# Row maxima, weight split and gate pieces in another order in a two-block transformer kernel

## The reference, cut to what matters

```
proj = rmsnorm(x) @ w_in                    # front columns, then 2 * 1024 gate columns
# mixer A: 8 heads on the 64 keys with the highest index score
score = where(causal, sum_h w_i * relu(q_i @ k_i.T), -inf)
idx   = top_k(score, 64)
o_a   = softmax(q_a @ k_a[idx] * scale + bias) @ v_a[idx]
# mixer B: 8 heads, three branches (compressed, selected, window), each with its gate
o_b   = g0 * softmax(q_b @ kc.T + bias) @ vc + g1 * softmax(q_b @ ks.T + bias) @ vs + g2 * (... kw, vw)
mix   = sigmoid(gate_a) * (o_a @ w_branch_a) + sigmoid(gate_b) * (o_b @ w_branch_b)
x     = x + mix @ w_out
```

## Time and profile before

| | us |
|---|---|
| three runs | 997.29, 998.59, 1000.55 |
| median | 998.59 |
| the profiled execution, its own time | 998.59 |
| its span in the trace | 996.8 |
| TensorE busy | 969.5 (97%) |
| VectorE busy | 576.7 (58%) |
| ScalarE busy | 495.0 (50%) |

### The profile page before, as it was taken

One profiled execution on the slowest core, in us unless ns is written; L12 is line 12 of the kernel. 1 busy time (PEld: TensorE's weight loads), 2 busy tenths in 40 slices (PEclk: granted clock), 3 DMA queues, 4 the chain that ended last, 5 costly groups with the idle time before them and its releaser, 6 DMA issues.

```text
span 996.8 us, 12359 instructions
## 1 busy us (share of the span) xinstructions
PE 969.5 (97%) x4788; PEld 779.8 (78%) x4788; DVE 576.7 (58%) x851; ACT 495.0 (50%) x686; POOL 5.7 (1%) x13
## 2 busy tenths in 40 slices
PE   6999999999999998999999999999999999999996
PEld 5777888888878875888888888877777788888885
DVE  5654756655356455475665437578874676545434
ACT  5664644434345564454444335556675464435332
POOL 0000000000000000000000001000000000000000
PEclk9999999999999998999999999999999999999998
DMA  9624545555445420454554548533224455545551
GB/s 324 213 86 148 208 172 190 189 174 195 180 169 177 161 85 1 172 209 168 195 184 172 225 174 313 193 132 127 85 96 158 169 172 185 191 170 190 196 184 42
DMA packets 25924, 168.76 MB, mean 169 GB/s; under 512 B 2792, under 2 KB 3798, under 8 KB 6679
## 3 DMA queue, kind: packets, MB, share of 16 engines
q1 hardware_dynamic: 24647, 163.57, 45.9%
q0 software_dynamic: 1232, 4.57, 1.2%
HBM read 167.05 MB, written 1.08 MB: 169 GB/s over the span
## 4 chain that ended last, share of the span: by engine, by line
PE 93%; DVE 3%; ACT 2%; DMA 1%; issue 1%; SPq 0%; ACTq 0%; DVEq 0%
PE ps L1437 79%; PE ps L1553 1%; PE ps L2033 1%; PE ps L1735 1%; PE ps L2044 1%; DMA x_sb<-in_x 1%; PE ps L2063 1%; PE ps L2132 1%; PE ps L1798 1%; PE ps L1627 1%; PE ps L1618 1%; PE ps L1513 1%; PE ps L1590 1%; PE ps L1856 1%; PE ps L1667 1%
## 5 line engine op out<-in xcount | busy, mean ns | idle before, releaser
L871 DVE TENSOR_TENSOR w_both<-raw,w_both 128x2048 fp32r<-128x2048 f32 x150 | 342.0, 2285 | 210.3 <-ACT w_both L409 210.2
L1437 PE MATMUL ps<-w_both,a_hi 128*128 128x512 f32 (+1 forms) x1536 | 416.0, 393 | 3.2 <-DVE m_lo L909 1.9
L409 ACT ACTIVATE w_both<-raw 128x2048 fp32r<-128x2048 f32 x150 | 286.4, 1916 | 188.8 <-DMA raw<-in_down 43.5
L1437 PEld LDWEIGHTS ps<-w_both,a_hi 128*128 128x128 f32 x1536 | 282.2, 189 | 63.7 <-issue 9.3
L1437 PE MATMUL ps<-w_both,a_lo 128*128 128x512 f32 (+1 forms) x768 | 235.6, 388 | 0.0
L1437 PEld LDWEIGHTS ps<-w_both,a_lo 128*128 128x128 f32 x768 | 143.9, 188 | 30.4
L1437 PE MATMUL ps<-w_both,h_hi 128*128 128x512 f32 x576 | 158.3, 396 | 0.0
L1437 PEld LDWEIGHTS ps<-w_both,h_hi 128*128 128x128 f32 x576 | 107.5, 188 | 25.6
L1437 PE MATMUL ps<-w_both,h_lo 128*128 128x512 f32 x288 | 90.5, 395 | 0.0
L1437 PE MATMUL ps<-w_both,m_hi 128*128 128x512 f32 x256 | 72.1, 404 | 2.3 <-ACT projA L490 1.4
L587 ACT ACTIVATE mlp_a<-ps,tiny 128x256 f32<-128x256 f32 x44 | 18.5, 471 | 98.2 <-PE ps L1437 98.2
(11 more groups left out here) (239 smaller groups left out, 686.3 us busy)
## 6 DMA issues: line engine op xcount, KB each, us to landing
raw<-in_a_gu SPq DMA_DIRECT2D x22, 1024.0 KB, 4.8
raw<-in_b_gu SPq DMA_DIRECT2D x22, 1024.0 KB, 4.8
raw<-in_up SPq DMA_DIRECT2D x16, 1024.0 KB, 4.8
raw<-in_down SPq DMA_DIRECT2D x16, 1024.0 KB, 4.8
raw<-in_a_down SPq DMA_DIRECT2D x11, 1024.0 KB, 4.8
raw<-in_b_down SPq DMA_DIRECT2D x11, 1024.0 KB, 4.7
raw<-in_front SPq DMA_DIRECT2D x8, 1024.0 KB, 5.1
raw<-in_gates SPq DMA_DIRECT2D x8, 1024.0 KB, 4.8
```

The costliest lines, as they stand in the source:

```text
L409: A_(ring(w_hi, us)[:, 0:n], ring(raw, us)[:, 0:n], ACT.Copy).then_inc(s_hi, 1)
L871: V.tensor_tensor(ring(w_lo, us)[:, 0:n], ring(raw, us)[:, 0:n], ring(w_hi, us)[:, 0:n].bitcast(fp32), ALU.subtract).then_inc(s_lo, 1)
L1437: ins = MM(ps[:, b + T, 0:wd], chT(parts[ap_], c, T), wp[wp_][:, off:off + wd], start=(c == first and pn == 0), stop=(c == last and pn == 2))
```

## The change

Four things move; no instruction is added or removed, and the line numbers behind the first edit on VectorE are shifted by one or two.
- ScalarE splits unit gates+2 ahead of the exponentials of the compressed scores, not behind them.
- VectorE does its half of that split, and two search rounds, ahead of pair 0's row maxima: the third round moves from the middle of the compressed softmax to behind it, the fourth comes from pair 1, and the split comes from behind pair 0's maxima.
- The other four rounds stand at pairs 0 to 3, not 2 to 5.
- TensorE does one gate piece behind the values at pairs 1, 2, 4, 5, 6, 8, 9 and 10; the number of pieces per pair is the same as before.

```diff
--- before.py
+++ after.py
@@ -753,9 +753,9 @@
             q_copy(14, ch(TT, 12, 2), 4, 1.0)
             front_block("front_a", 0, U0["front_a"] + 2, 0)
             q_copy(15, ch(TT, 14, 2), 7, 1.0)
+            split_hi(U0["gates"] + 2)
             act.wait_ge(s_clm, 1)
             A_(pc_v, pc_v, ACT.Exp).then_inc(s_cex, 1)
-            split_hi(U0["gates"] + 2)
 
             def gate_block(b):
                 act.wait_ge(s_mm, U0["gates"] + 2 * b + 2)
@@ -1259,7 +1259,7 @@
             ins.then_inc(s_cau, 1)
             split_lo(U0["gates"] + 1)
             dve.wait_ge(s_cau, 1)
-            for _k in range(2):
+            for _k in range(TOPS_AHEAD // 2):
                 replaced = top_taken(top_found())
 
             dve.wait_ge(s_clg, 1)
@@ -1278,8 +1278,6 @@
             link(V.tensor_reduce(cmx, pc_v, AX.X, ALU.max))
             link(V.tensor_scalar(cmx, cmx, -1.0e20, None, ALU.max))
             V.tensor_tensor(pc_v, pc_v, per_row(cmx), ALU.subtract).then_inc(s_clm, 1)
-            for _k in range(2, TOPS_AHEAD):
-                replaced = top_taken(top_found())
             dve.wait_ge(s_cex, 1)
             link(V.tensor_reduce(csum, pc_v, AX.X, ALU.add))
             link(V.tensor_scalar(csum, csum, 1.0e-30, None, ALU.max))
@@ -1288,6 +1286,9 @@
             link(V.tensor_tensor(crec.rearrange("p (t n) -> p t n", t=2), crec.rearrange("p (t n) -> p t n", t=2),
                                  gb.rearrange("p (t n) -> p t n", t=2)[:, :, 0:8], ALU.mult))
             V.tensor_tensor(pc_v, pc_v, per_row(crec), ALU.mult).then_inc(s_cp, 1)
+            split_lo(U0["gates"] + 2)
+            for _k in range(TOPS_AHEAD // 2, TOPS_AHEAD):
+                replaced = top_taken(top_found())
             for p in range(n + 3):
                 if p < n:
                     u = CAUSAL_PAIRS[p]
@@ -1306,8 +1307,6 @@
                     found = top_found()
                     if k + 1 < TOP_STEPS[p]:
                         replaced = top_taken(found)
-                if p == 0:
-                    split_lo(U0["gates"] + 2)
                 if p - 1 in GATE_SPLIT:
                     split_lo(U0["gates"] + GATE_SPLIT[p - 1])
                 if p < n:
@@ -2086,7 +2085,7 @@
             left = list(range(7, 32))
             for p in range(n):
                 pair_transposes(p)
-                first, then = PIECES.get(p, (2, 0))
+                first, then = PIECES.get(p, (1, 1))
                 for _k in range(first):
                     gate_piece(left.pop(0))
                 pair_values(p)
@@ -2185,9 +2184,9 @@
 INDEX_BANK = (6, 4, 5)
 GATE_EMPTY = {2: 0, 5: 1, 9: 2, 13: 3}
 GATE_SPLIT = {1: 3, 3: 4, 5: 5, 7: 6, 9: 7, 10: 8, 11: 9}
-TOP_STEPS = {p: 1 for p in range(1, 6)}
-TOPS_AHEAD = 3
-PIECES = {0: (1, 0), 1: (3, 0), 2: (3, 0)}
+TOP_STEPS = {0: 1, 1: 1, 2: 1, 3: 1}
+TOPS_AHEAD = 4
+PIECES = {0: (1, 0), 1: (2, 1), 2: (2, 1), 3: (2, 0), 7: (2, 0), 11: (2, 0)}
 assert TOPS_AHEAD + sum(TOP_STEPS.values()) == S // 4 // 8
```

## The result

| | before | changed |
|---|---|---|
| median of nine runs, us | 999.53 | 1004.84 |
| lowest to highest | 995.64 to 1000.83 | 1002.56 to 1008.28 |
| profiled execution: span | 996.8 | 1002.2 |
| mean granted clock | 0.994 | 0.994 |

The ratio is 1.0067, 95% interval 1.0049 to 1.0086: the change makes the kernel about 0.7% slower. It is not the quotient of the two medians, 1.0053: 24 runs of the changed kernel are on record, from 1002.56 to 1008.38 us with a mean of 1005.5, and single runs of either kernel lie up to 5 or 6 us apart. 1006.6 us was forecast, with 1003.0 to 1009.8.

The account below looks back on a forecast made before the run. TensorE, busy 969.5 of 996.8 us, was taken to set the end. Wait 4.75, next wait 0.15, joints 1.7, late copy 0.1 and clock 1.3 sum to 8.0 us on 998.6: 1006.6 us, range 1003.0 to 1009.8.

Parts of the forecast that it names:

- The wait: Ahead of pair 1's logits: TensorE waits 4.75 us for VectorE's late row maxima of pair 0.
- The next wait: Ahead of pair 2's logits: TensorE waits for pair 1's maxima, 0.15 us more, at most 0.3.
- The joints: Gate pieces split around the values at 8 pairs: 0.24 us each with logits behind, 0.13 without, 1.7 in all.
- The sign that the prediction gave for this stretch: From pair 0's transposes to the first branch product: 1.5 to 2.5 us more than before.
- The rival of free joints: Gate pieces at all pairs: a piece costs the same anywhere, so 1004.9 us in total; chance 0.14.
- The late copy at pair 4: Values at pair 4: one piece covers too little of ScalarE's copy behind a split, a wait of 0.1 us.
- The clock: Behind the hole ahead of pair 1's logits: the granted clock falls, costing 1.3 us, ends 0 and 3.4.
- the row's 1.6: Loss read from the profile before at 380.40 to 384.00 us: a hole, then 3.40 us at clock 0.50.
- the third rival: Gate pieces at all pairs: joints are free by the skill's page, so 1004.9 us in total; chance 0.14.
- The first rival: Gate pieces' new places hide TensorE's weight-load gaps and give back 4.4 us: 1000.5 us, not slower; chance 0.05.
- the second: Pair 1's logits: the wait for pair 0's maxima doesn't come, only the joints count, 1000.4 us; chance 0.07.
- the fourth: ScalarE's work no longer fits before the copies ahead of the values; 8 pairs wait 0.5 us more each: 1010.6; chance 0.08.

Follow-up runs that it names:

- The split alone: Kernel before with only the split of unit gates+2 moved ahead, on ScalarE and VectorE: wait of 2.03 us at pair 1; pair 0's logits to its transposes 14.81 us.
- the rounds alone: Kernel before with only the search rounds moved ahead of pair 0's maxima: waits of 0.81 us at pair 1 and 1.44 at pair 2.
- the hole filled: Changed kernel plus 20 matmuls that nobody reads ahead of pair 1's logits: 1005.54 us; with such matmuls in the memory attention too, 1000.59 us.
- part 2 alone: Kernel before with only the new table of gate pieces: 999.21 against 996.87 us, ratio 1.0008; with unread matmuls in the memory attention, 996.08 against 994.92 us.
- the keepers: 20 unread matmuls in four holes of the memory attention: kernel before 995.33 us, ratio 0.9978; in the last set 994.92, changed kernel 1002.87 us.
- part 1 alone: Changed kernel with the old table of gate pieces: ratio 1.0077 to the kernel before; A (pair 0's logits to its transposes) 19.04 us, wait 4.81.
- the set without the other spread: Last set, unread matmuls in the memory attention of all four kernels: before 994.92 us, changed 1002.87, changed with hole filled 1000.59, new piece table only 996.08.

## Why the prediction was right, and where it was off

**The wait** (4.75 us forecast, 4.82 measured). Every step of the working is in the new timeline: from ScalarE's split to its exponentials 1.80 (1.81), from the softmax to the split 1.47 (1.46), the split 2.20 (2.21), the two rounds 2.75 (2.75), the maxima 1.19 (1.19). The point that carried it is that VectorE's queue is in order and stood 1.6 us ahead of TensorE, so that all beyond that was paid in full. The split alone and the rounds alone gave the waits that the same sum gives, 2.0 and 0.8.

**The next wait** (0.15 forecast) did not show. The low clock behind the hole held TensorE back by more than that. With the hole filled, at full clock, there are 0.2 us between the last queries and pair 2's logits that the old kernel does not have there (691.34 to 692.07, 0.73 against 0.53); that is the term, hidden in the changed kernel.

**The joints** (1.7 forecast, 1.07 measured with the 0.13 wait in it; 1.16 in whole time). This is the term that was mis-sized. At pairs 1 and 2 a split group costs the forecast 0.24 (4.53 against 4.29 for three pieces), at pair 4 0.35 with the wait. At pairs 5, 6 and 8 it costs 0.02 to 0.04: what follows there is the mask product, which uses the full array, so that the two pieces cost only 0.12 to 0.14 more and the product, behind a piece, gives back 0.1. The prediction took these three for pairs with logits behind, though the mask product stands between. At pairs 9 and 10 the next transposes give back 0.06 of 0.14. Together 0.48 + 0.35 + 0.08 + 0.16 = 1.07. The sign that the prediction gave for this stretch, 1.5 to 2.5 us more, failed. The rival of free joints is refuted too: the stretch grew by 1.05 us with part 2 alone, and the whole time by 1.16 with the keepers in. "TensorE: Matmul & The Clock Gate" ("Wait — 56ns, not 53.3ns?") of the Trainium skill gives the spacing of matmuls in a row, by which a piece is estimated at 1.29 us. That is below the least of all spacings of pieces measured, 1.36, and lone pieces take up to 1.60.

**The late copy at pair 4** (0.1 forecast). The values start at 719.45 where the piece alone would let them at 719.32, just behind a copy that ends at 719.40. ScalarE's timeline:

```profile
716.73 1.91 ACT L409 ACTIVATE w_both<-raw 128x2048 fp32r<-128x2048 f32 x1
718.53 0.87 ACT L770 ACTIVATE pb<-ps 128x384 f32<-128x384 f32 x2
```

and TensorE's:

```profile
717.75 1.17 PE L1436 MATMUL ps<-w_both,a_hi 128*128 128x512 f32 x4
718.76 0.62 PE L1436 MATMUL ps<-w_both,a_lo 128*128 128x512 f32 x2
719.45 0.65 PE L2059 MATMUL ps<-pct,cw 15*64 15x256 f32 x4
```

**The clock** (1.3 forecast from 0 to 3.4; 1.58 in the profile, 2.28 over the runs). The mechanism was right and the size drawn low. The reason given for taking less than the row's 1.6, that the fall may lie partly in the hole, need not hold: with the keepers a fall inside the hole was followed by a low clock for the whole of the next 5 us, at a cost of 2.6 (6.88 against 4.25 from pair 1's logits to pair 2's). In part 1 alone the clock fell just ahead of the end of the hole as well (0.93 in the microsecond before it), and the cost was 1.5 (A 19.04, less 12.71 and the wait of 4.81). What decides between the two is open.

**The sum** was 8.0; the changed kernel costs 7.5 by its stretches and 7.95 in the set without the other spread. That it comes so close is in part luck: the joints were put 0.6 too high, the low clock 0.3 to 1.0 too low. By the plain medians the change costs only 5.3 us (1004.84 less 999.53), and 1004.84 is nearest to the 1004.9 of the third rival, whose mechanism the runs refute. Such medians depend on how many low stretches the memory attention had in the runs that were drawn; of the single runs only the mean clock is on record. The first rival (time given back at the joints) and the second (no wait) are refuted; of the fourth (cover too thin) only the 0.13 at pair 4 is true.

## What to carry to other kernels

Where one engine has no wait in a stage, a reordering of the others has no wait to remove there; find each engine's slack at the places where the full one takes its results, and price the reordering by what exceeds that slack. Slack is spent once, so two moves that are cheap alone can be dear together. And a hole in a matmul stream can be paid with more than its length, as the one of 4.8 us was here and the one of 2.0 was not: look at the granted clock in the stretch behind it, and at small waits elsewhere that do the same. Matmuls whose results nobody reads, put into such holes, gave back 2.3 us at the one and 2.2 at the four.

## What the runs showed of the hardware that was not expected

A stage with four holes of 0.9 to 1.7 us within 11 us decides the spread of a program of 1000 us: without its low clock the runs of the kernel before lie within 1.5 us, with it within 7. The mean clocks agree: of the 23 runs, those at 0.998 took 994.00 to 995.68 us and those at 0.991 took 999.93 to 1000.88. The same busy time led to different clocks: 1.47 us busy of 3.20 was followed by a stretch at 0.50 in the kernel before, and 1.45 of 3.20 by one at 1.00 in the changed kernel.

The kernel before:

```profile
387.40:390.60 3.20, 1.47 (x11) 0.72 (x10) 1.42 (x3) 1.50 (x4) 0.00 (x0) 1.00 0.00 0
390.80:394.20 3.40, 3.40 (x9) 2.63 (x10) 2.20 (x1) 2.97 (x2) 0.00 (x0) 0.50 0.00 0
```

The changed kernel (its next row, at 1.00, is shown with the result):

```profile
387.40:390.60 3.20, 1.45 (x10) 0.90 (x11) 1.42 (x3) 1.66 (x4) 0.00 (x0) 1.00 0.03 5
```

Behind waits of 2.03 and of 0.81 and 1.44 us at the pairs' logits the clock stayed at full speed. Behind waits of 1.50 and 1.37 us with only one set of logits between them it fell to 0.52. With the 4.8 us it fell in all three profiles that had it: the changed kernel, part 1 alone, and the changed kernel with keepers. Which of two equal stretches is followed by the low clock stays open.
